# An unused gap ahead of the weight halves widened from 120 to 216 words

## The chip, the cores and the metric

One core of a Trainium2 chip. The metric is the device time of one execution in microseconds; lower is better. Times are medians of several executions, and one further execution was taken with the hardware profiler.

## The reference, cut to what matters

Two transformer blocks run one after the other on 256 tokens of width 1024, all in float32.

The first block: a modulation `silu(c) @ ada_w`; an RMS norm with scale and shift; `h @ w_in` into retention and stick-breaking attention heads; an output projection; then a layer of 16384 single-neuron experts:

```python
qry = (ht @ w_query).reshape(T, 8, 2, 128)
sub_scores = einsum('thpc,hpkc->thpk', qry, sub_keys)      # top 16 of 128, twice, then 16 of 256
a = einsum('pd,ped->pe', xb, expert_down[ib])
act = gelu(a) * gate
y = einsum('pe,ped->pd', act, expert_up[ib])
```

The second block: `h @ w_in_2` into compressed, selected and windowed attention and a short convolution, an output projection `w_o_2`, then `square(relu(h @ w_up_2)) @ w_down_2` with a hidden width of 4096.

## The kernel before, in words

**Products in halves.** No large float32 product is done in one pass. ScalarE rounds a weight tile into `w_hi` (type float32r, L1203), VectorE subtracts that from the tile into `w_lo` (L1672); the activations are kept as `hT_hi` and `hT_lo` in the same way, or `a_hi` (L1200) and `a_lo` (L2132). TensorE then adds three products: high by high, high by low, low by high. The first argument of `matmul` is the stationary operand (at most 128 columns, loaded by a weight load ahead of the matmul), the second the moving one (streamed, up to 512 columns).

**Weights.** SyncE brings 2 MB tiles of 4096 words per partition into two slots of `wring`. A tile is split in four parts `u` of 1024 words; `w_hi` and `w_lo` hold those four parts. A part is written again once TensorE has used it (`parts_used`).

**Three forms of product.**
- Column form, `column_part` (L635 to L637) and `column_half` (L624 to L626): 128 columns of a weight half are stationary, `hT[:, k, :]` with 256 columns moves. Used for the query projection (`wq`, 4 tiles), the expert projection with all 16384 experts (`dn`, 32 tiles) and the up projection (`up`, 8 tiles). A tile is 96 matmuls.
- Token form, `token_part` (L613 to L615), `out_part`, `out_block` and `wo_part`: 128 columns of `hT` are stationary, a weight half moves with 512 columns, or with 280 in the last chunk of `w_in_2`. Used for both input and both output projections.
- Row form, `row_part` (L647 to L649): 128 columns of `a_hi` or `a_lo` are stationary, a weight half with 512 columns moves. Used for the expert output (`ex`, 32 tiles) and the down projection (`down`, 8 tiles). In the gated part the blocks of `up` and `down` alternate.

**The dense experts.** All experts are computed and weighed by a dense table of gates. For the second 128 tokens GpSimd scatters the gates into DRAM with 128 indirect DMAs (L1624), 16 for a head, each head after the landings of the one before. For the first 128 tokens TensorE makes them from one-hot vectors: `spread_products` (L925), four matmuls with 128 stationary and 256 moving columns out of the same buffer `onehot`, placed in the column blocks from tile 19 of `dn` on; VectorE takes them out (L2100), ScalarE stores them (L1397). Before the first tile of `ex`, SyncE waits for all gates to be stored (L527 and the lines after it), reads them back, and VectorE multiplies them in (L2124, L2127).

**Where the buffers lie.** `two_blocks` declares its tensors of on-chip memory one behind another; each takes its words per partition, rounded up to 32 bytes. In order, with words per partition: const 1249, x_tok 2048, h_tok 2048, hT_hi 2048, hT_lo 2048, pages 4096, spare 2048, late 1536, diag 512, modc 48, gains 40, small 448, gap_of_weights 120, wring 8192, w_hi 4096, w_lo 4096, gap_of_acts 16, adab 48, trig 128, zeros 256, posi 2, posf 2, st 160, gateT_hi 128, cbias 4, w2 256, b2 128, besti 512, gatec 48, mx 16, sm 16, kcn 128, kcq 64, kcst 4, kcmpT 64, peT 32, and then a_hi 1024, a_lo 1024 and onehot 6144. The first starts at byte 16512. `peer_arena` takes the place of `onehot`, `arena` that of `a_hi` and all behind it. The two gaps are read and written by nothing. By these sizes, modulo 512 bytes:

| buffer | place modulo 512 |
|---|---|
| hT_hi, hT_lo | 32 |
| w_hi, w_lo | 96 |
| a_hi, a_lo, onehot | 32 |

```python
pe.matmul(o, hi[:, k, :], hT_hi[:, k, :], ...)         # column form: w_hi stationary
pe.matmul(o, hT_hi[:, k, t], hi[:, kk, :], ...)        # token form: hT_hi stationary
pe.matmul(o, a_hi[:, u, t], hi[:, half, :], ...)       # row form: a_hi stationary
```

Of the kernel before, what the change touches and what calls it, by code (L numbers as in the profile page):

```python
# [39 lines left out]
P = 128  # L40
# [185 lines left out]
def two_blocks(nc, a, out, stop=None):  # L226
    ctx = ExitStack()
    with ctx:
        def sb(name, shape, dt=F32):
            return ctx.enter_context(nc.sbuf_tensor(name, shape, dt))  # L230
# [15 lines left out]
        modc = sb("modc", [P, 6 * KC])  # L246
        gains = sb("gains", [P, 5, KC])
        small = sb("small", [P, 7, HD])
        sb("gap_of_weights", [P, 120])
        wring = sb("wring", [P, RING, SLOT])  # L250
        w_hi = sb("w_hi", [P, PARTS, PART], F32R)
        w_lo = sb("w_lo", [P, PARTS, PART], F32R)
# [2176 lines left out]
```

How the kernel before makes its waits and increments, by code:

```python
    def __call__(self, ins):  # L215
        self.n += 1
        ins.then_inc(self.sem, 1)
        self.eng.wait_ge(self.sem, self.n)
# [196 lines left out]
        def stands(eng, kind, j):  # L415
            n = NTH[kind, j]
            if kind in RAW:
                eng.wait_ge(w_used, RAW_BEFORE[n + 1])
            else:
                eng.wait_ge(parts_used, SPLIT_BEFORE[n + 1])
# [1 line left out]
        def slot_left(eng, n):  # L423
            if STREAM[n][0] in RAW:
                eng.wait_ge(w_used, RAW_BEFORE[n + 1])
            else:
                eng.wait_ge(split_lo, SPLIT_BEFORE[n + 1])
# [30 lines left out]
        @block.sync  # L459
# [46 lines left out]
            weights(RING)  # L506
            sp.dma_start(spare[:, :], a["decay"]).then_inc(ld_decay, 16)
            sp.dma_start(rgain, a["ret_gain"].partition_broadcast(P)).then_inc(ld_decay, 16)
            weights(RING + 1)
            sp.dma_start(peT[:, :, :], a["pe"]).then_inc(ld_cmp, 16)
            sp.dma_start(cbias[:, :, :], a["b_cmp1"]).then_inc(ld_cmp, 16)
            sp.dma_start(w2[:, :, :, :], a["w_cmp2"].rearrange("v (f p) d -> p v f d", p=P)).then_inc(ld_cmp, 16)
            sp.dma_start(b2[:, :, :], a["b_cmp2"]).then_inc(ld_cmp, 16)
            for n in range(RING + 2, NTH["wq", RING]):
                weights(n)
            sp.wait_ge(S["h_ready"], 4)
            sp.dma_start(keys.rearrange("p c n -> p (c n)"), a["keys"]).then_inc(ld_keys, 16)
            def first_gates_back(turn):
# [81 lines left out]
            def split_landed(n, u):  # L601
                pe.wait_ge(split_lo, SPLIT_BEFORE[n] + u + 1)
```

## Time and profile before

| | |
|---|---|
| median of 3 executions | 1321.92 us (1310.96 to 1323.77) |
| profiled execution | 1314.53 us |
| its span, first to last instruction | 1312.7 us |
| TensorE matmul busy | 1258.1 us |
| VectorE busy | 990.8 us |
| ScalarE busy | 729.1 us |
| GpSimd busy | 307.4 us |
| mean granted clock of TensorE | 0.980 |

PE is the matmul side of TensorE, PEld its weight loads, DVE VectorE, ACT ScalarE, POOL GpSimd, SP SyncE. A matmul's duration in the trace holds its way through the array, so durations of neighbours overlap; what a matmul costs is the time from its start to the next one's start.

### The profile page before, as it was taken

Reading aid. Unit: us, or ns where it says so; the run is one execution under the profiler, and the core shown is the slowest. Engines: PE = TensorE matmul, PEld = TensorE weight load, DVE = VectorE, ACT = ScalarE, POOL = GpSimd, SP = SyncE. Lnnn points to the kernel's source line nnn. Section 1 sums busy time; section 2 is a strip of 40 time slices with the busy share of each in tenths; the row PEclk is TensorE's granted clock in tenths of the full one; section 3 lists DMA queues with packets and bytes.
Section 4 is the critical chain, followed back from the end, with each engine's and each line's share of the span. In section 5 each row is a group of like instructions: output and inputs, shape, how many; then the busy total and the mean of one; then the engine's idle time right before and its main releaser. Section 6 shows DMA issues by size and latency. Waiting matters only on the chain.

```text
span 1312.7 us, 19845 instructions
## 1 busy us (share of the span) xinstructions
PE 1258.1 (96%) x7918; PEld 1122.3 (85%) x7918; DVE 990.8 (75%) x1720; ACT 729.1 (56%) x1130; POOL 307.4 (23%) x186
## 2 busy tenths in 40 slices
PE   3799979999999999998999999999989998999998
PEld 3678869999999999998888888888867687899997
DVE  6989998899999889984677777777776465755555
ACT  3566534555555699983444444444455456554443
POOL 0125010278675867570000000000000013000000
PEclk8899989999999999999999999999999998999999
DMA  9964669977778778889888888887645432355552
GB/s 368 360 231 154 213 255 366 319 203 224 243 250 268 213 240 249 289 282 352 308 287 291 286 284 292 285 291 282 231 161 184 164 143 98 143 184 195 191 191 94
DMA packets 138575, 317.10 MB, mean 242 GB/s; under 512 B 24816, under 2 KB 71153, under 8 KB 132595
## 3 DMA queue, kind: packets, MB, share of 16 engines
q1 hardware_dynamic: 101394, 265.42, 56.4%
q0 software_dynamic: 23072, 16.86, 6.9%
q10 hardware_dynamic: 14016, 33.56, 6.7%
q8 instruction: 63, 1.03, 0.3%
q14 instruction: 30, 0.24, 0.0%
HBM read 280.61 MB, written 35.20 MB: 241 GB/s over the span
## 4 chain that ended last, share of the span: by engine, by line
PE 63%; POOL 18%; DMA 6%; DVE 5%; issue 5%; ACT 2%; SPq 0%; ACTq 0%; DVEq 0%; POOLq 0%
POOL gates_of_second L1624 18%; PE ps L648 11%; PE ps L647 11%; PE ps L649 11%; DMA gates_of_second<-late 5%; PE ps L613 3%; PE ps L615 3%; PE ps L614 3%; PE ps L635 3%; PE ps L636 3%; PE ps L637 3%; PE ps L977 1%; DVE arena L1752 1%; DVE w_lo L1672 1%; DVE pages L1752 1%
## 5 line engine op out<-in xcount | busy, mean ns | idle before, releaser
L1672 DVE TENSOR_TENSOR w_lo<-wring,w_hi 128x1024 fp32r<-128x1024 f32 (+1 forms) x404 | 492.7, 1226 | 166.4 <-ACT w_hi L1203 162.2
L1203 ACT CAST w_hi<-wring 128x1024 fp32r<-128x1024 f32 (+1 forms) x404 | 419.1, 1044 | 239.6 <-PE ps L637 143.1
L635 PE MATMUL ps<-hT_hi,w_hi 128*128 128x256 f32 x1344 | 373.5, 278 | 0.0
L637 PE MATMUL ps<-hT_hi,w_lo 128*128 128x256 f32 x1344 | 373.1, 278 | 0.0
L636 PE MATMUL ps<-hT_lo,w_hi 128*128 128x256 f32 x1344 | 373.1, 278 | 0.0
L1624 POOL DMA_INDIRECT gates_of_second<-late x128 | 250.0, 1953 | 141.0 <-issue 51.9
L635 PEld LDWEIGHTS ps<-hT_hi,w_hi 128*128 128x128 f32 x1344 | 254.1, 189 | 0.3
L636 PEld LDWEIGHTS ps<-hT_lo,w_hi 128*128 128x128 f32 x1344 | 252.3, 188 | 0.3
L637 PEld LDWEIGHTS ps<-hT_hi,w_lo 128*128 128x128 f32 x1344 | 252.3, 188 | 0.0
L647 PE MATMUL ps<-w_hi,a_hi 128*128 128x512 f32 x624 | 245.6, 394 | 3.8 <-DVE w_lo L1672 3.8
L648 PE MATMUL ps<-w_lo,a_hi 128*128 128x512 f32 x624 | 246.7, 395 | 0.0
L649 PE MATMUL ps<-w_hi,a_lo 128*128 128x512 f32 x624 | 243.8, 391 | 0.0
L1200 ACT CAST a_hi<-peer_arena 128x256 fp32r<-128x256 f32 x128 | 52.0, 407 | 183.5 <-PE ps L649 94.4
L647 PEld LDWEIGHTS ps<-w_hi,a_hi 128*128 128x128 f32 x624 | 117.8, 189 | 31.1 <-issue 4.0
L649 PEld LDWEIGHTS ps<-w_hi,a_lo 128*128 128x128 f32 x624 | 117.8, 189 | 26.1
L648 PEld LDWEIGHTS ps<-w_lo,a_hi 128*128 128x128 f32 x624 | 118.0, 189 | 23.9
L613 PE MATMUL ps<-w_hi,hT_hi 128*128 128x512 f32 (+1 forms) x208 | 84.1, 404 | 17.8 <-DVE w_lo L1672 16.6
L2132 DVE TENSOR_TENSOR a_lo<-peer_arena,a_hi 128x256 fp32r<-128x256 f32 x128 | 54.3, 424 | 51.8 <-ACT a_hi L1200 51.8
L1628 POOL MEMSET pages<- 2x512 f32 x1 | 0.5, 515 | 385.7 <-PE ps L751 385.7
L615 PE MATMUL ps<-w_hi,hT_lo 128*128 128x512 f32 (+1 forms) x208 | 81.3, 391 | 0.0
L614 PE MATMUL ps<-w_lo,hT_hi 128*128 128x512 f32 (+1 forms) x208 | 81.3, 391 | 0.0
L613 PEld LDWEIGHTS ps<-w_hi,hT_hi 128*128 128x128 f32 x208 | 40.1, 193 | 28.3 <-issue 19.9
(322 smaller groups left out, 1489.5 us busy)
## 6 DMA issues: line engine op xcount, KB each, us to landing
wring<-in_peer_down SPq DMA_DIRECT2D x32, 2048.0 KB
wring<-in_peer_up SPq DMA_DIRECT2D x32, 2048.0 KB
wring<-in_w_in SPq DMA_DIRECT2D x12, 2048.0 KB
pages<-in_ada_t POOLq DMA_DIRECT2D x32, 512.0 KB, 5.3
acts_by_expert<-pages ACTq DMA_DIRECT2D x32, 512.0 KB
peer_arena<-acts_by_expert SPq DMA_DIRECT2D x32, 512.0 KB, 8.6
wring<-in_w_up SPq DMA_DIRECT2D x8, 2048.0 KB
wring<-in_w_down SPq DMA_DIRECT2D x8, 2048.0 KB
```

The lines of the kernel that those rows point to most:

```text
L613: pe.matmul(o, hT_hi[:, k, t], hi[:, kk, :], start=(k == 0), stop=False)
L614: pe.matmul(o, hT_hi[:, k, t], lo[:, kk, :], start=False, stop=False)
L615: mm = pe.matmul(o, hT_lo[:, k, t], hi[:, kk, :], start=False, stop=(k == KC - 1))
L635: pe.matmul(o, hi[:, k, :], hT_hi[:, k, :], start=(k == 0), stop=False)
L636: pe.matmul(o, hi[:, k, :], hT_lo[:, k, :], start=False, stop=False)
L637: mm = pe.matmul(o, lo[:, k, :], hT_hi[:, k, :], start=False, stop=(k == KC - 1))
L647: pe.matmul(o, a_hi[:, u, t], hi[:, half, :], start=first, stop=False, skip_group_check=True)
L648: pe.matmul(o, a_hi[:, u, t], lo[:, half, :], start=False, stop=False, skip_group_check=True)
L649: mm = pe.matmul(o, a_lo[:, u, t], hi[:, half, :], start=False, stop=last, skip_group_check=True)
L1203: act.copy(split_part(kind, w_hi, u, width(kind, j)), part_of(kind, wring[:, n % RING, :], u, width(kind, j))).then_inc(split_hi, 1)
L1624: pool.indirect_dma_start(gates_second, bass.IndirectOffsetOnAxis(ap=place_of[:, head, k:k + 1], axis=0), gate_of[:, 1, head, k:k + 1], No ...
L1672: dve.tensor_tensor(lo, part_of(kind, wring[:, n % RING, :], u, width(kind, j)), hi, ALU.subtract)\
```

## The change

One declaration grows by 96 words, 384 bytes per partition. Every tensor declared behind it lies 384 bytes further; nothing else is changed.

```diff
         small = sb("small", [P, 7, HD])
-        sb("gap_of_weights", [P, 120])
+        sb("gap_of_weights", [P, 216])
         wring = sb("wring", [P, RING, SLOT])
         w_hi = sb("w_hi", [P, PARTS, PART], F32R)
         w_lo = sb("w_lo", [P, PARTS, PART], F32R)
```

The distance from hT to the weight halves is +64 bytes before and -64 after, modulo 512. The distance from the weight halves to a_hi and a_lo stays what it was.

## Rows read from the trace of the kernel before

**Rows 1.** The page: busy time by engine, and the costliest groups of matmuls.
```profile
PE 1258.1 (96%) x7918; PEld 1122.3 (85%) x7918; DVE 990.8 (75%) x1720; ACT 729.1 (56%) x1130; POOL 307.4 (23%) x186
...
L635 PE MATMUL ps<-hT_hi,w_hi 128*128 128x256 f32 x1344 | 373.5, 278 | 0.0
...
L647 PE MATMUL ps<-w_hi,a_hi 128*128 128x512 f32 x624 | 245.6, 394 | 3.8 <-DVE w_lo L1672 3.8
...
L613 PE MATMUL ps<-w_hi,hT_hi 128*128 128x512 f32 (+1 forms) x208 | 84.1, 404 | 17.8 <-DVE w_lo L1672 16.6
```
**Rows 2.** Windows: us, busy PE, PEld, DVE, ACT, POOL (instructions), granted clock, DMA, GB/s.
```profile
254.00:466.30 212.30, 212.30 (x1876) 212.30 (x1875) 198.15 (x621) 126.62 (x144) 153.67 (x80) 1.00 0.76 234
466.30:614.50 148.20, 148.20 (x1258) 148.20 (x1257) 120.66 (x106) 123.04 (x289) 94.79 (x48) 1.00 0.87 281
...
1131.00:1312.00 181.00, 177.53 (x1160) 160.96 (x1160) 103.05 (x116) 84.94 (x113) 0.00 (x0) 1.00 0.47 171
```
**Rows 3.** Timeline of TensorE, column form: first and thirteenth start.
```profile
299.99 0.28 PE L635 MATMUL ps<-hT_hi,w_hi 128*128 128x256 f32 x1
...
301.35 0.28 PE L635 MATMUL ps<-hT_hi,w_hi 128*128 128x256 f32 x1
```
**Rows 4.** Timeline of TensorE around the first one-hot products.
```profile
466.34 0.64 PE L925 MATMUL ps<-onehot 128*128 128x256 f32 x4
466.82 0.28 PE L635 MATMUL ps<-hT_hi,w_hi 128*128 128x256 f32 x1
...
469.53 0.28 PE L637 MATMUL ps<-hT_hi,w_lo 128*128 128x256 f32 x1
```
**Rows 5.** Timeline of TensorE, row form: first and thirteenth start.
```profile
799.87 0.39 PE L647 MATMUL ps<-w_hi,a_hi 128*128 128x512 f32 x1
...
802.62 0.39 PE L647 MATMUL ps<-w_hi,a_hi 128*128 128x512 f32 x1
```
**Rows 6.** Timeline of TensorE: first starts of three neighbouring blocks in the gated part.
```profile
1154.78 0.40 PE L647 MATMUL ps<-w_hi,a_hi 128*128 128x512 f32 x1
...
1165.98 0.28 PE L635 MATMUL ps<-hT_hi,w_hi 128*128 128x256 f32 x1
...
1176.88 0.39 PE L647 MATMUL ps<-w_hi,a_hi 128*128 128x512 f32 x1
```
**Rows 7.** Timeline of TensorE, token form, 512 columns: first and tenth start.
```profile
80.56 0.39 PE L613 MATMUL ps<-w_hi,hT_hi 128*128 128x512 f32 x1
...
82.63 0.39 PE L613 MATMUL ps<-w_hi,hT_hi 128*128 128x512 f32 x1
```
**Rows 8.** Timeline of TensorE, token form, 280 columns: first and twentieth start.
```profile
1077.95 0.29 PE L614 MATMUL ps<-w_lo,hT_hi 128*128 128x280 f32 x1
...
1080.36 0.29 PE L615 MATMUL ps<-w_hi,hT_lo 128*128 128x280 f32 x1
```
**Rows 9.** Chain of waits: start, us, what (16 transposes).
```profile
72.46 1.75 PE ps L733 x16
```
**Rows 10.** Timeline of TensorE from projection to expert output; window behind it.
```profile
614.44 0.28 PE L637 MATMUL ps<-hT_hi,w_lo 128*128 128x256 f32 x1
618.52 0.76 PE L647 MATMUL ps<-w_hi,a_hi 128*128 128x512 f32 x1 [3.81 <-DVE w_lo L1672]
...
618.60:622.50 3.90, 3.90 (x9) 3.03 (x10) 3.90 (x6) 3.19 (x5) 0.00 (x0) 0.50 0.95 343
```
**Rows 11.** Chain of waits between 591 and 619 us.
```profile
591.95 12.04 DMA gates_of_second<-late
...
604.50 9.85 DMA peer_arena<-gates_of_first
```
**Rows 12.** The scatter's group; timeline at the store of the last one-hot products.
```profile
L1624 POOL DMA_INDIRECT gates_of_second<-late x128 | 250.0, 1953 | 141.0 <-issue 51.9 <-DVEq L2025 49.2 <-DMA gates_of_second<-late 39.9
...
590.57 0.33 ACTq L1397 DMA_DIRECT2D gates_of_first<-spare  x1
```
**Rows 13.** Groups by form: sums of the modulation on VectorE.
```profile
L1752 DVE SCALAR_TENSOR_TENSOR pages<-pages,arena 128x1024 f32<-128x1024 f32 x36 | 45.0, 1279 | 0.8 <-DMA pages<-in_ada_t 0.8
```

## The prediction, made before the change was run

> **What bounds the kernel now.** I read the page first: TensorE is busy for 96% of the span, no other engine for more than 75% [rows 1]. Then the windows by stage, for where that busy time is real: in the two stretches of the expert projection and in the gated one the matmul engine has no idle time or almost none [rows 2]. The chain of waits on the page names GpSimd for 18%; its place is checked below. The change moves buffers and alters no instruction, so all that it can touch is the pace of instructions that read or write the moved buffers. For that I read starts in the timeline and divide by the number of matmuls between them.
>
> What "distance" means is worked out from the declared sizes (each tensor in the order of its declaration, rounded up to 32 bytes): hT_hi and hT_lo lie at 32 modulo 512, w_hi and w_lo at 96, a_hi and a_lo at 32, the one-hot buffers at 32. After the change all that is declared behind the gap lies 384 bytes further: weight halves at 480, a at 416, hT still at 32. So three kinds of matmul must be told apart, by stationary less moving operand:
> - column form (L624 to L626, L635 to L637): weight half stationary, hT moving, 256 columns: +64 now, -64 after. 1344 x 3 [rows 1] and 192 in halves, 4224 in all.
> - token form (L613 to L615, and the output projections): hT stationary, weight half moving, 512 columns (280 in the last chunk): -64 now, +64 after. 208 x 3 [rows 1] and 192, 816 in all.
> - row form (L647 to L649): a stationary, weight half moving, 512 columns: -64 now and after, since both move together. 624 x 3 = 1872 [rows 1].
>
> **The paces that the trace shows.** The granted clock is 1.00 in these stretches [rows 2], the upper level of 2.4 GHz, at which 256 columns take 106.7 ns and 512 take 213.3.
> - Column form, first part: 12 matmuls in 1.36 us, 113.3 ns, 6.6 over the columns' time [rows 3].
> - One-hot products, 256 columns, distance 0: 4 in 0.48 us, 120 ns, 13.3 over. And the columns behind them do not go back: 23 in 2.71 us, 117.8 ns, 11.1 over, on the same instruction at the same clock [rows 4]. They stay there until the end of the projection. I call this the disturbed pace.
> - Row form: 12 in 2.75 us, 229.2 ns, 15.9 over [rows 5]. The one row block behind disturbed columns takes 11.20 us for 48, 233.3 ns, 20 over, and the 96 columns behind it take 10.90 us, 113.5 ns each: the first pace again [rows 6].
> - Token form, 512 columns: 9 in 2.07 us, 230 ns, 16.7 over [rows 7]; 280 columns: 19 in 2.41 us, 126.8 ns, 10.1 over 116.7 [rows 8].
>
> So no distance but +64 shows an excess below 10 ns. The steps between the paces are near 6.7 ns, the time of 16 columns or 64 bytes (113.3 and 120.0; the others lie between whole steps, as if some matmuls of three paid one more). I read this as reads of the stationary and the moving operand that meet now and then and cost one such step each; the sign and size of the distance decide how often. That reading is an inference: length and distance are confounded, as all rows at -64 are longer than 256 columns.
>
> **The change part by part.** Instructions added, removed or moved in order: none; waits: none; DMA sizes: none. What it costs is a number of matmuls by a change of pace. For the column form at -64 the trace has no row of 256 columns. From below: 109 ns, the pace of the transposes (16 in 1.75 us) [rows 9], which is 4 ns under now. From above: the 20 ns of the disturbed row form, 126.7 ns, 13.4 over now. Between: the 10.1 ns of the 280-column row at that very distance give 116.8; the 15.9 of 512 columns 122.6. I take 120.0, one step over now, which lies between these two nearest and is what 256 columns do at distance 0.
>
> Step by step, at 120.0:
> 1. Query projection, 384 matmuls x 6.7 ns = +2.6 us. It delays the start of the top-k and so of the GpSimd scatter by as much.
> 2. Expert projection, 32 x 96 = 3072 matmuls. The first one-hot product starts at 466.34; before it lie 19 blocks and 120 matmuls, 1944 x 6.7 = 13.0 us. Behind it 1128 x 2.2 (120.0 less 117.8) = 2.5 us. Together 15.5.
> 3. Not all of that counts. The last column matmul starts at 614.44, the first row matmul only at 618.52 [rows 10]: it waits for the scattered gates, which land at 604.0, are read back until 614.35 and then multiplied and split [rows 11]. The scatter's 128 instructions take 250 us of GpSimd, with 51.9 us of issue and 39.9 us of landings between them, and once begun wait for nothing of TensorE's [rows 12]; so this end stays where it is (but for step 1). Of the 15.5 us, 4.0 are idle time filled. TensorE also no longer cools: now the clock is at 0.50 behind the gap [rows 10], some 8 matmuls at 427 in place of 229 ns and a slower first one, 1.9 us. Net +9.6. What is late next is TensorE itself: the first half's gates, whose last product starts at 588.64 and whose last store is issued at 590.57 [rows 12], move by the same 15.5 to some 606, are back some 12 us later and split by 622, still ahead of the last column matmul at 630.
> 4. Up projection: seven blocks of 96 and two halves that make another. 576 at the first pace x 6.7 = 3.9, 192 at the disturbed one x 2.2 = 0.4: +4.3 us.
> 5. Row form: distance unchanged, 0. If it takes over the disturbed pace from the columns without an idle time between, 1536 x 4.2 = 6.4 us more; that is kept for the range.
> 6. Token form turns to +64, where only 256 columns are shown (6.6 over). Bounds: nothing, and 9.3 ns each. 144 of the 816 fall into the first stretch, where TensorE is idle 8 of 46 us for want of weights and the clock stands at 0.85 [rows 2], and count as hidden; 672 x 9.3 = 6.2 us at most. I take half, -3.1.
> 7. VectorE's sums of the modulation read pages and a row in the arena, whose distance changes too: 1279 ns with both, 1218 within the arena [rows 13], 36 x 61 ns = 2.2 us either way, mostly beside DMA. Taken as 0. ScalarE's and VectorE's splits read and write buffers that move together.
>
> Sum: 2.6 + 9.6 + 4.3 - 3.1 = +13.4 us. The profiled execution took 1314.5 us (span 1312.7), so it would be 1327.9. The median shown is 1321.9, 7.4 above that execution, and the prediction is set on it: 1335.3.
>
> The Trainium skill speaks against the whole: "SBUF — State Buffer", section "Who interferes with whom", gives TensorE two read ports of its own, one for the moving operand and one for the weight load, independent of each other, and says that PE never waits on anyone. The rows do not agree: one and the same instruction runs at 113.3 and at 117.8 ns at full clock, and which it is hangs on what ran before. By that rule the sum is 0; its case is the first rival.
>
> **The rivals.**
> - *The distance does not matter at +-64* (same bank or not is all that counts, or only the row's length makes 512 columns costlier). For it: row and token form run alike at the same length; the disturbed pace comes and goes without any change of distance. Against it: the jump from 6.6 to 10.1 ns between 256 and 280 columns. Time: 1321.9, give or take 5.
> - *Worse than one step*: two steps per column matmul, 126.7 ns. Then 5.1 + (25.9 + 10.0 - 5.9) + (7.7 + 1.7) = 44.5 us, with the rows of step 5 some 51: 1366 to 1373. For it only that the disturbed row form has 20 ns over. A weaker form, the disturbed pace throughout (117.8), gives 1.7 + (8.7 - 5.9) + 2.6 = +7.1, less the tokens' 3.1.
> - *Faster*: at -64 the columns do not fall into the disturbed pace, and the tokens gain in full. The first brings nothing in the expert projection, because the gates are the end there [rows 10, 11]; it brings 192 x 4.5 = 0.9 in the up projection and 48 x 4.2 = 0.2 behind it; with 6.2 from the tokens -7.3: 1314.6. If columns came down to 109 ns as well, another 384 x 4.3 + 768 x 4.3 = 5.0: 1309.7. It decides where the columns' pace does not rise above 113.3. The trace has nothing at 256 columns of this kind under 113.3 ns, which is why this side is short.
> - *The gap does not move anything*: excluded, as the offsets follow the declarations.
>
> **How the numbers follow.** One step (116.8 to 122.6 ns, +6 to +25 us): 0.40. No change: 0.35. Stronger: 0.15. Faster: 0.10. A measurement tells about 1% (13 us) from no change. Slower by more than that are the stronger case and two thirds of the forecast's (the sum itself lies at the bound, with the rows' pace taken over it is +20): 0.15 + 0.26 = 0.41. Faster by more needs nearly all of the third rival: 0.05. The rest, 0.54, is within 1%. Range: from 1313 (the faster case cut at its middle) to 1362 (the stronger one cut near its lower end); the forecast's own is 1328 to 1347.
>
> **What the profile after would show.** Starts of L635 to L637 between 300 and 440 us 120 ns apart in place of 113; the end of the projection near 632, and no idle time ahead of the first L647, whose clock stays at 1.00; L647 still 229 apart; L613 under 230. If columns stand at 113.3, the forecast falls with its main term. If they stand at 120 and the time is the same, then the wait for the gates or the tokens took it back.

## The result and the profile after

The changed kernel takes 1328.55 us (median of 12 executions, 1324.96 to 1334.44); the kernel before, timed beside it, 1315.01 (12, 1310.96 to 1325.47). The ratio is 1.0095, with a 95% interval of 1.007 to 1.012: slower by about 13 us. The prediction was +13.4 us on the median then known, 1321.9; timed beside the changed kernel, that median was 1315.0, so the time came out below the forecast 1335.3 while the difference came out as forecast.

The page after, against [rows 1]: TensorE is busy for the same share, and 89% of the chain that ended last is now TensorE's (before it was 63%, and GpSimd's scatter had 18%).

```profile
PE 1278.6 (96%) x7918; PEld 1134.7 (85%) x7918; DVE 991.6 (74%) x1720; ACT 728.5 (55%) x1130; POOL 297.8 (22%) x186
...
PE 89%; DVE 5%; DMA 3%; ACT 2%; issue 1%; ACTq 0%; SPq 0%; DVEq 0%
```

The timeline of TensorE after, column form (start, us, instruction), against [rows 3]:

```profile
304.75 0.28 PE L635 MATMUL ps<-hT_hi,w_hi 128*128 128x256 f32 x1
...
306.17 0.28 PE L635 MATMUL ps<-hT_hi,w_hi 128*128 128x256 f32 x1
```

12 matmuls in 1.42 us are 118 ns (117.8 over longer stretches). That is not the 120.0 that was forecast, but the pace that the prediction calls "disturbed", and it holds in all column tiles. There is one exception, the 120 column matmuls behind the transposes of the gates (L912):

```profile
463.06 0.49 PE L912 MATMUL ps<-const,late 128*128 128x128 f32 x3
463.31 0.36 PE L635 MATMUL ps<-hT_hi,w_hi 128*128 128x256 f32 x1
463.51 0.28 PE L636 MATMUL ps<-hT_lo,w_hi 128*128 128x256 f32 x1
...
464.64 0.28 PE L637 MATMUL ps<-hT_hi,w_lo 128*128 128x256 f32 x1
```

Ten in 1.13 us are 113 ns, on the same instruction, operands and distance as a moment before. So one stream can run at 113.3 or at 117.8, and the distance alone does not name the pace. Below, "state" means which of its two paces a stream runs at.

Row form and token form after, against [rows 5] and [rows 7]:

```profile
799.96 0.40 PE L647 MATMUL ps<-w_hi,a_hi 128*128 128x512 f32 x1
...
802.76 0.40 PE L647 MATMUL ps<-w_hi,a_hi 128*128 128x512 f32 x1
...
81.27 0.39 PE L613 MATMUL ps<-w_hi,hT_hi 128*128 128x512 f32 x1
...
83.37 0.40 PE L613 MATMUL ps<-w_hi,hT_hi 128*128 128x512 f32 x1
```

Rows: 12 in 2.80 us, 233.3 ns, though their distance is the old one. Tokens, now at +64: 9 in 2.10 us, 233.3 ns, where [rows 7] gave 230 at -64.

Between projection and expert output, against [rows 10] and [rows 11], timeline and then chain:

```profile
624.69 0.28 PE L637 MATMUL ps<-hT_hi,w_lo 128*128 128x256 f32 x1
627.54 0.47 PE L647 MATMUL ps<-w_hi,a_hi 128*128 128x512 f32 x1 [2.57 <-DVE w_lo L1672]
```

```profile
599.06 0.48 PE ps L925 x4
...
599.56 1.24 DVE spare L2100
...
600.82 9.86 DMA gates_of_first<-spare
...
610.76 12.60 DMA peer_arena<-gates_of_first
```

The idle time ahead of the first row matmul did not close; it went from 4.0 to 2.8 us. Its end moved with the columns: the gates of the first 128 tokens come out of one-hot products that stand among them, and their store (9.86 us) and their way back (12.60 us) take 22 us.

### The profile page after: what moved, and what is told of

It is laid out like the page before. It is cut to its first block, busy times and chain, and to the rows that moved or that the text cites. A ratio compares the mean times of both kernels' runs of the same rounds, so it can differ in the third digit from the quotient of the medians.

```text
span 1332.6 us, 19845 instructions
## 1 busy us (share of the span) xinstructions
PE 1278.6 (96%) x7918; PEld 1134.7 (85%) x7918; DVE 991.6 (74%) x1720; ACT 728.5 (55%) x1130; POOL 297.8 (22%) x186
## 4 chain that ended last, share of the span: by engine, by line
PE 89%; DVE 5%; DMA 3%; ACT 2%; issue 1%; ACTq 0%; SPq 0%; DVEq 0%
PE ps L636 11%; PE ps L635 11%; PE ps L637 11%; PE ps L647 11%; PE ps L649 11%; PE ps L648 11%; PE ps L613 4%; PE ps L614 3%; PE ps L615 3%; PE ps L925 1%; PE ps L977 1%; DVE w_lo L1672 1%; DVE pages L1752 1%; DVE arena L1752 1%; DMA peer_arena<-gates_of_first 1%; PE ps L775 1%
## 5 line engine op out<-in xcount | busy, mean ns | idle before, releaser
L635 PE MATMUL ps<-hT_hi,w_hi 128*128 128x256 f32 x1344 | 375.9, 280 | 1.2 <-DVE w_lo L1672 1.2
L1624 POOL DMA_INDIRECT gates_of_second<-late x128 | 240.2, 1877 | 129.7 <-DMA gates_of_second<-zeros 52.3
L635 PEld LDWEIGHTS ps<-hT_hi,w_hi 128*128 128x128 f32 x1344 | 252.4, 188 | 1.6 <-issue 1.3
L649 PE MATMUL ps<-w_hi,a_lo 128*128 128x512 f32 x624 | 247.9, 397 | 0.0
```

The costliest lines, as they stand in the source:

```text
L635: pe.matmul(o, hi[:, k, :], hT_hi[:, k, :], start=(k == 0), stop=False)
L649: mm = pe.matmul(o, a_lo[:, u, t], hi[:, half, :], start=False, stop=last, skip_group_check=True)
L1624: pool.indirect_dma_start(gates_second, bass.IndirectOffsetOnAxis(ap=place_of[:, head, k:k + 1], axis=0), gate_of[:, 1, head, k:k + 1], No ...
```

## The experiments

Three theories stood at the start: *distance* (the difference modulo 512 between the places of the two operands decides), *place* (the absolute addresses decide) and *entry* (the start of a block sets a state that is then kept). Paces are averages from starts in the timelines. Where a group of instructions is quoted, it is the one in a window of fixed length, and the number behind the "x" tells the pace, because a slower stream starts fewer matmuls in the same time:

- 310 to 440 us, each line of the column form: 383 starts at 113.3 ns, 368 or 369 at 117.8, 361 or 362 at 120.0.
- 700 to 900 us, each line of the row form: 291 or 292 starts at 228.9 ns, 286 or 287 at 233.3, 294 or 295 at 226.7.

### Is it the distance? (e1, e2)

```diff
-        sb("gap_of_weights", [P, 120])
+        sb("gap_of_weights", [P, 88])
```

> The gap ahead of the weight halves is 88 words instead of 120: hT to weight halves is -64 modulo 512, as with 216 words, but everything behind the gap lies 128 bytes lower instead of 384 higher. Theory (the pace hangs on the distance modulo 512): the same as the changed kernel, columns at 117.8 ns in the expert projection from its start, 1.0095 of the kernel before. Rival (the absolute place of the buffers, or how far they lie apart, sets it): columns at 113.3 ns up to the first one-hot product and a ratio within 0.997 to 1.003, or some third pace.

Measured: ratio 1.0092 (1.0061 to 1.0123), 1325.7 to 1334.8 us. The groups:

```profile
L635 PE MATMUL ps<-hT_hi,w_hi 128*128 128x256 f32 x368 | 102.7, 279 | 0.0
...
L647 PE MATMUL ps<-w_hi,a_hi 128*128 128x512 f32 x292 | 114.5, 392 | 0.0
```

Columns at 117.8, with 113.4 behind L912, as in the changed kernel; the rows at 228.9. A gap that is narrower than before, with the same distance modulo 512 as the changed kernel's, does the same, so it is not the size of the gap. But the weight halves lie at 480 modulo 512 here too, so this run does not part distance from place modulo 512. The next one does.

```diff
+        sb("gap_of_turned", [P, 96])
         hT_hi = sb("hT_hi", [P, KC, T], F32R)
```

> The 96 extra words stand ahead of hT instead of behind it: hT, weight halves, a and one-hot all lie 384 bytes further, and every distance among them is that of the kernel before (+64 from hT to the weight halves). Theory (distance modulo 512): columns at 113.3 ns up to the first one-hot product, ratio 1.000 within 0.3%. Rival (absolute place modulo 512): columns at 117.8 ns, ratio 1.009.

Measured: ratio 1.0014 (0.9967 to 1.0061), 1312.1 to 1328.5 us. The profiled execution (1321.9):

```profile
L636 PE MATMUL ps<-hT_hi,w_hi 128*128 128x256 f32 x368 | 103.4, 281 | 0.0
```

The time is what the theory says. The row is what the rival says: 117.8 ns at a distance of +64. One profile could not settle it, so the kernel before was profiled again (next section), and that took the row's weight away: the kernel before shows 117.8 there too. What is left of this run is for the distance. Its lowest time is 1312.1 us, and all 27 executions of the changed kernel, of the 88-word gap and of e10 below (all at -64) lie above 1324.5. And in its gated part the columns between row blocks run at 113.3 (12 in 1.36 us), where the changed kernel has 117.8 (12 in 1.41 us); timeline of this run, then of the changed kernel:

```profile
1197.22 0.28 PE L636 MATMUL ps<-hT_hi,w_hi 128*128 128x256 f32 x1
...
1198.58 0.28 PE L636 MATMUL ps<-hT_hi,w_hi 128*128 128x256 f32 x1
```

```profile
1188.02 0.28 PE L635 MATMUL ps<-hT_hi,w_hi 128*128 128x256 f32 x1
...
1189.43 0.28 PE L635 MATMUL ps<-hT_hi,w_hi 128*128 128x256 f32 x1
```

### How fixed is the pace? (e5, e6)

Nothing is edited.

> The kernel before once more, unchanged, for a second profile of it. Theory (at a distance of +64 the columns have two paces, and which one an execution gets is not fixed by the program): columns of the expert projection at 113.3 or 117.8 ns from the start; a change against the first profile would prove it. Rival (the entry into the block fixes it): 113.3 up to the first one-hot product, 117.8 behind it, as before, to a few ns.

```profile
L635 PE MATMUL ps<-hT_hi,w_hi 128*128 128x256 f32 x369 | 103.9, 281 | 0.0
```

Measured: 1326.09 us (one execution), columns at 117.8 in all whole tiles up to the gated part. The same program, with the same inputs and distance, had them at 113.3 in the execution of 1314.5 us. The first column tile is where they part, timeline of this execution:

```profile
187.39 0.36 PE L624 MATMUL ps<-hT_hi,w_hi 128*128 128x256 f32 x1 [2.17 <-issue]
187.59 0.28 PE L625 MATMUL ps<-hT_lo,w_hi 128*128 128x256 f32 x1
...
188.19 0.42 PE L624 MATMUL ps<-hT_hi,w_hi 128*128 128x256 f32 x1
```

and of the first profiled execution of the kernel before:

```profile
187.31 0.55 PE L624 MATMUL ps<-hT_hi,w_hi 128*128 128x256 f32 x1 [1.83 <-issue]
187.66 0.42 PE L625 MATMUL ps<-hT_lo,w_hi 128*128 128x256 f32 x1
```

This execution enters the tile at the upper clock level (granted clock 0.96 up to 188.2 us, matmul durations of 0.28), falls to the lower one (0.50, durations of 0.42) for 3 us and comes back at 117.8. The first one enters at the lower level (0.50) and comes up at 113.3. So the entry differs, but the clock at the entry is not what decides. Three other kernels with +64 or +320 (e2, e4 and e12) enter at the lower level as well and come up at 117.8. This is e12:

```profile
187.13 0.55 PE L624 MATMUL ps<-hT_hi,w_hi 128*128 128x256 f32 x1 [3.10 <-issue]
187.49 0.41 PE L625 MATMUL ps<-hT_lo,w_hi 128*128 128x256 f32 x1
```

Nor is the first entry the last word: e2 and e12 ran half a tile at 113.3 (between 196 and 202 us) before they settled at 117.8.

> The changed kernel once more. Theory (at -64 the columns have the slow pace alone, while the rows, whose distance is the old one, still have two): columns at 117.8 ns again but for the 120 behind the transposes; rows of the expert output at 229 or 233 ns, the execution 6 to 7 us shorter if 229. Rival (the slow rows belong to the change): 233 again.

```profile
L635 PE MATMUL ps<-hT_hi,w_hi 128*128 128x256 f32 x368 | 102.8, 279 | 0.0
...
L647 PE MATMUL ps<-w_hi,a_hi 128*128 128x512 f32 x292 | 113.4, 388 | 0.0
```

Measured: 1328.34 us (one execution); columns as in the other execution, rows at 228.9. So the slow rows of the first profile after, 359.8 us for the expert output against 353.0 here, do not belong to every execution of the changed kernel. Whether the change makes them possible is open: no profile of a kernel with the rows' distance at -64 and the columns' at +64 had them in the expert output.

### Other distances (e3, e7, e12)

Gaps of 104, 168 and 184 words in the same declaration.

> The gap is 104 words: hT to weight halves is 0 modulo 512; weight halves to a unchanged. Theory (the distance decides, and equal places meet most): columns at 120 ns, the pace that the one-hot products had at distance 0 before, up to 4032 x 6.7 = 27 us less what the wait for the gates hides (6), ratio 1.010 to 1.017. Rival (any distance but a lucky one gives the disturbed pace of 117.8): ratio 1.009 as at -64. Rival (nothing but the entry decides): 113.3 in places.

> The gap is 168 words: hT to weight halves is 256 modulo 512, as far from equal as can be, for both signs. Theory (the slow pace comes from reads at near places, within 64 bytes): columns at 113.3 ns throughout or faster, tokens at 227 or less, ratio at or below 1.000 (0.993 to 1.002). Rival (+64 is a lucky place among many bad ones): columns at 117.8 or 120, ratio 1.009 to 1.012.

> The first gap is 184 words: hT to weight halves is +320 modulo 512, which is +64 modulo 256. 0 and 256 had the same 120.0 ns. Theory (the distance counts modulo 256): as the kernel before, columns with two paces, 113.3 or 117.8 by execution, times spread over 1310 to 1328 us, ratio 1.000 within 0.5%. Rival (modulo 512, or the distance's size only): columns at 117.8 or 120 always, ratio 1.009 to 1.012.

L635 in the window, for 0, 256 and 320:

```profile
L635 PE MATMUL ps<-hT_hi,w_hi 128*128 128x256 f32 x362 | 102.4, 283 | 0.0
```

```profile
L635 PE MATMUL ps<-hT_hi,w_hi 128*128 128x256 f32 x362 | 102.6, 283 | 0.0
```

```profile
L635 PE MATMUL ps<-hT_hi,w_hi 128*128 128x256 f32 x368 | 103.6, 281 | 0.0
```

At 0: ratio 1.0112 (1.0051 to 1.0174), columns at 120.0 everywhere, tokens at 227.4. At 256: 1.0119 (1.0051 to 1.0187), the same 120.0 and 227.5, so the theory that far apart is good is refuted. At 320: 1.0002 (0.9961 to 1.0043), times from 1309.9 to 1324.1 as the kernel before has them, 117.8 in the projection of this execution and 113.6 in the gated part. So 0 and 256 go together, and 64 and 320 do: as far as these two pairs go, the distance counts modulo 256, with +64 and -64 still apart.

### The rows' distance (e4, e11)

```diff
-        sb("gap_of_acts", [P, 16])
+        sb("gap_of_acts", [P, 48])
```

> Kernel before with the second gap at 48 words instead of 16: a lies at +64 from the weight halves instead of -64 (stationary less moving operand in the row form), columns and tokens unchanged. Theory (sign counts as stationary less moving, +64 is the good side, as for the columns): rows drop from 229 to some 220 ns, 1872 x 9 = 17 us faster, ratio 0.987. Rival (the length of 512 columns makes the excess, not the distance): rows at 229, ratio 1.000. Rival (weight halves 64 bytes above the activations is good whatever the role): rows at 233 or over, 8 us slower, ratio 1.006.

```profile
L635 PE MATMUL ps<-hT_hi,w_hi 128*128 128x256 f32 x369 | 103.7, 281 | 0.0
...
L647 PE MATMUL ps<-w_hi,a_hi 128*128 128x512 f32 x287 | 113.1, 394 | 0.0
```

Measured: ratio 1.0118 (1.0054 to 1.0182); all rows at 233.1 to 233.3. The sign that is good for the columns costs the rows; that is the pace of the last of the three theories. The time is twice what it gives (1.006), so the rows are not all of it. The columns, whose distance is still +64, ran at 117.8 up to the one-hot products and at 113.3 behind them, and in the gated part their blocks alternated between 113.5 and 117.8, where the kernel before has 113.6 in all blocks but the first. So what the rows do changes the state of the columns behind them.

> The kernel before with the second gap at 32 words: a lies 0 from the weight halves instead of -64, the columns' distance stays +64. Theory (512 columns behave as the token form did: 229 at -64, 233 at +64, 227.4 at 0): rows at 227.4 ns always, 1872 x 1.5 to 5.9 = 3 to 11 us faster than the kernel before whose rows have two paces, ratio 0.993 to 0.998, columns with two paces still. Rival (equal places are worst, as for the columns): rows at 233 or more.

 (the same line with 32 words)

```profile
L647 PE MATMUL ps<-w_hi,a_hi 128*128 128x512 f32 x294 | 114.5, 389 | 0.0
```

Measured: ratio 1.0003 (0.9971 to 1.0035), rows at 226.7. The pace came nearly as expected (227.4), the time did not. The gain over 228.9 is 1872 x 2.2 = 4.1 us. Against it stand the columns of the gated part, which ran at 117.8 in all blocks of the profiled execution and at 113.6 in all but the first before: 576 x 4.2 = 2.4 us lost. What is left, under 2 us, is too small for the spread of both kernels (1309 to 1321 and 1311 to 1327). Behind the one-hot products the pace of the columns changed back and forth between 113 and 117.8.

### Starts in the middle of 64 bytes (e8)

```diff
+        sb("gap_of_turned", [P, 8])
         hT_hi = sb("hT_hi", [P, KC, T], F32R)
```

> Eight words (32 bytes) of gap ahead of hT: hT, weight halves, a and one-hot start at 64, 128, 64 and 64 modulo 512 instead of 32, 96, 32 and 32, all distances as before. Theory (a read goes in pieces of 64 bytes, and a start in the middle of one costs one more piece for each matmul): columns lose one step of 6.7 ns down to the cost of a transpose (109 ns), rows about as much: 4224 x 4.2 + 1872 x 4 to 6.7 = 25 to 30 us, less some for the gates' wait, ratio 0.98 to 0.985. Rival (only distances matter): ratio 1.000 within 0.3%, the same paces.

```profile
L636 PE MATMUL ps<-hT_hi,w_hi 128*128 128x256 f32 x383 | 105.9, 276 | 0.0
...
L648 PE MATMUL ps<-w_hi,a_hi 128*128 128x512 f32 x292 | 113.4, 388 | 0.0
```

Measured: ratio 0.9976 (0.9934 to 1.0018), the paces of the kernel before to a tenth of a nanosecond. The theory of a piece lost at the start is refuted. The absolute places rest on the first byte of the layout, which no run shows; but the two kernels lie 32 bytes apart, so they cannot both start in the middle of 64.

### Can the state be set? (e9, e10)

Both edits are made in the changed kernel, in `by_columns`, behind `bank = free_banks(n)`; the tile's own matmuls overwrite what the transposes write.

```diff
+                if (kind, j) == ("dn", 5):
+                    for _ in range(3):
+                        pe.transpose(psf[:, bank * 512:bank * 512 + P], ident, ident)
```

> The changed kernel (-64) with three transposes of the identity ahead of tile 5 of the expert projection, into a bank that the tile's first matmul overwrites; nothing else. Theory (the pace is a state that the entry into a block sets and that then keeps; behind such transposes the columns of the changed kernel ran at 113.4 ns): columns from tile 5 to the first one-hot product at 113.4, some 1340 x 4.4 = 5.9 us off the projection, ratio to the kernel before 1.004 to 1.006. Rival (something else of the stage sets it, such as what the other engines do): 117.8 as before, ratio 1.0095.

Timeline of TensorE around the three:

```profile
301.37 0.28 PE L636 MATMUL ps<-hT_lo,w_hi 128*128 128x256 f32 x1
301.49 0.28 PE L637 MATMUL ps<-hT_hi,w_lo 128*128 128x256 f32 x1
301.61 0.49 PE L726 MATMUL ps<-const 128*128 128x128 f32 x3
301.85 0.36 PE L635 MATMUL ps<-hT_hi,w_hi 128*128 128x256 f32 x1
302.06 0.28 PE L636 MATMUL ps<-hT_lo,w_hi 128*128 128x256 f32 x1
...
302.96 0.28 PE L635 MATMUL ps<-hT_hi,w_hi 128*128 128x256 f32 x1
```

Ahead of them 117.8; behind them eight in 0.90 us, and 1344 matmuls at 113.3, up to the transposes of the gates. Behind those it went back to 117.8, where the changed kernel had gone the other way. Ratio 1.0043 (1.0005 to 1.0081), where the changed kernel has 1.0095. This shows that at -64 too the columns can run at 113.3, that what TensorE did before decides it, and what it is worth: 1344 x 4.5 = 6.0 us, and by the ratios about 7.

```diff
+                if kind != "dn" or j < 2:
+                    pe.transpose(psf[:, bank * 512:bank * 512 + P], ident, ident)
```

> The changed kernel (-64) with one such transpose ahead of every tile in column form but tiles 2 and later of the expert projection. Theory (entry sets the pace): columns at 113.4 in the query projection, in tiles 0 to 18 and in the up projection, where 117.8 stood; 2100 x 4.4 = 9 us, 2 of them hidden by the wait for the gates, and 672 x 4.4 = 3 us in the up projection, less 12 transposes of 0.11 us: ratio 1.001 to 1.003. Rival: one transpose is too little or another state follows: 117.8 and 1.010.

```profile
L635 PE MATMUL ps<-hT_hi,w_hi 128*128 128x256 f32 x368 | 102.8, 279 | 0.0
```

Measured: ratio 1.0115 (1.0059 to 1.0172), 117.8 in every whole column tile, behind the gates' transposes too. The rival holds: one transpose does not do what three did. Which sequence leads to which state is open.

## Why the prediction came out right

The direction was right, and so was its kind: the distance slows the columns. That the sum was right too (+13.4 against about +13 measured) is luck, as most of its terms were not. Starts from the timelines, in us:

| | before | before again | after | after again |
|---|---|---|---|---|
| first column matmul | 187.3 | 187.4 | 188.7 | 188.9 |
| first one-hot product | 466.3 | 476.3 | 477.0 | 477.4 |
| last column of the projection | 614.4 | 624.4 | 624.7 | 625.1 |
| first row matmul | 618.5 | 627.5 | 627.5 | 628.2 |
| last row of the expert output | 972.7 | 980.6 | 987.3 | 981.2 |
| first column of the gated part | 1131.2 | 1142.8 | 1148.9 | 1142.8 |
| last matmul | 1309.1 | 1320.7 | 1329.0 | 1322.9 |

The steps of the sum, "before" against "after again" (rows at 228.9 in both):
- Steps 1 and 2, the columns up to the end of the projection: forecast 2.6 + 15.5, measured +9.0. The term was mis-sized: at -64 the columns take 117.8, not 120.0. 120.0 belongs to 0 and 256. The mechanism, a whole step that the distance adds, is right for those two. The weaker form in the second rival (the disturbed pace throughout) named the pace; its sum, +7.1 less 3.1 for the tokens, is +4.0, under a third of what was measured.
- Step 3, what the wait hides: forecast -5.9, measured -1.0 of idle time and -1.1 behind it. What failed is that the first half's gates would be "back some 12 us later" than their store and so ahead of the last column. From the issue of the store at 600.82 to the end of the read it took 22.5 us: 9.86 for the store to land and 12.60 for the read. The 12 us are about the read alone. So once the columns are slow, this path ends last and moves with them. The kernel before does the same in the execution whose columns ran at 117.8, with 10.90 and 11.82 us and an idle time of 3.1, chain of e5:

```profile
600.55 10.90 DMA gates_of_first<-spare
611.53 11.82 DMA peer_arena<-gates_of_first
```

- Step 4, the up projection: forecast +4.3, measured +2.3 (177.9 to 180.1 us), again 117.8 for 120.0.
- Step 5, the rows: forecast 0 with 6.4 kept for the range. Right in kind. One execution after had all rows of the expert output at 233.3, which is the case that the range was kept for. The kernel before has that pace in one block of its gated part [rows 6].
- Step 6, the tokens: forecast -3.1. The sign was wrong: 233.3 at +64 for 229, which by 672 x 4.3 costs 2.9 us at most. It rested on "no distance but +64 shows an excess below 10 ns", which confounded length and distance, as the text said. At 512 columns 0 is best, -64 next, and +64 worst, level with the 233.3 that -64 can show.

The stages that hold the tokens grew by more than that, +1.6 us up to the first column and +3.1 from the last row to the gated part, and neither is shown to be the tokens'. The first column matmul starts 0.1 us behind the end of a split on VectorE (L1699), and this split comes late in the changed kernel, but not in e9, whose tokens lie at +64 as well. Chain of the kernel before, of the changed one and of e9, where the line number is three higher:

```profile
185.98 1.23 DVE hT_lo L1699
```

```profile
187.36 1.23 DVE hT_lo L1699
```

```profile
186.03 1.22 DVE hT_lo L1702
```

The later stage takes 158.5 us before and 161.6 after, but 162.3 in "before again", whose tokens run at 229. So how much of the 4.7 us is the distance's is not shown.

Sum of what was measured: 9.0 - 1.0 - 1.1 + 2.3 + 4.7 = 13.9, against 13.8 between the spans (1312.7 and 1326.5). Column terms that were too large made up for a wait that hid less than forecast and for two token stages that grew where they were to shrink.

What neither the forecast nor its rivals had is that the kernel before comes in two kinds. The execution profiled first had its columns at 113.3; another had them at 117.8 and took 1326.1 us, 2.2 less than the changed kernel's 1328.3. In the last comparison 16 of its 25 executions lay below 1320 and 9 above 1321; of the changed kernel's 12 none lay below 1324.9. The profiled pairs put the cost of the change at 2 us against the kind with 117.8 (the gated part, 180.1 us for 177.9) and 14 against the kind with 113.3. So, mostly, the change takes the second kind away. That the unprofiled executions divide by the pace of the columns is inferred from their times.

The Trainium skill's rule that TensorE waits for nobody at its two read ports ("SBUF — State Buffer", "Who interferes with whom") was set at 0.35 as "no change". The runs do not agree with it here: nothing but the width of a gap takes the columns from 113.3 or 117.8 ns (+64) to 120.0 (0 and 256).

Open: what sets the state at an entry, and which reads, if any, meet. The steps fit 16 columns' time, but the run that moved all starts by 32 bytes changed nothing. Other distances between 64 and 256 were not tried.

## What to carry to other kernels

Before a layout is judged by one profile, profile it twice and compare start-to-start times of the same instruction at the same granted clock: a stream of matmuls that never waits had two paces here, 4% apart. Where weight loads and moving operands come from buffers at fixed distances, the distance is a setting like another, and in these runs the best one depended on the role of the operands and the number of columns, so measure each form by itself. Where a result is computed among the matmuls and they wait for it later, it moves when they get slower, so an idle time ahead of that wait cannot be counted as room for them. Price its whole way, the store and the read.

## What the runs showed of the hardware that was not expected

- Matmuls with 256 moving columns, stationary less moving place: +64 and +320, 113.3 or 117.8 ns; -64, 117.8, and 113.3 where transposes had gone ahead; 0 and 256, 120.0. With 512: -64, 228.9 or 233.3; +64, 233.3; 0, 226.7 (row form) and 227.4 (token form); 256, 227.5.
- A state lasts: 1728 matmuls in a row ran at either pace, while the other engines worked beside them. It changed where TensorE itself did something else in between: three transposes, or a block of another form. It did not change each time.
- All operands moved by 32 bytes together: no effect within 0.1 ns.
